# Weighing the sampled values: stationary pages or stationary probabilities

## The reference, cut to what matters

```
s = einsum('bqhd,bqkhd->bqhk', q, k_sel) * HEAD_DIM ** -0.5     # k_sel: chosen past tokens and the new one
p = softmax(where(valid, s, -inf))
o = einsum('bqhk,bqkhd->bqhd', p, v_sel)                        # per sample b and head h: 64 values
y = concatenate([o * silu(ga), ...])                            # then the output projection and the residual
```

## Time and profile before

| | us |
|---|---|
| median of 3 runs | 876.19 (873.66 to 878.19) |
| profiled execution | 876.71 |
| its span | 875.4 |
| TensorE matmul / weight load busy | 805.3 / 637.6 |
| VectorE / ScalarE / GpSimd busy | 609.3 / 328.0 / 333.1 |
| mean granted TensorE clock | 0.945 |

### The profile page before, as it was taken

How to read it: one execution, slowest core, us unless ns; L and a number is a source line. 1 busy time by engine, 2 the same in 40 slices (tenths; PEclk the granted TensorE clock), 3 DMA queues, 4 the chain that set the end, 5 groups by cost and what they waited for, 6 DMA issues and landing times. The chain is left out here.

```text
span 875.4 us, 13288 instructions
## 1 busy us (share of the span) xinstructions
PE 805.3 (92%) x4620; PEld 637.6 (73%) x4620; DVE 609.3 (70%) x1432; ACT 328.0 (37%) x830; POOL 333.1 (38%) x317
## 2 busy tenths in 40 slices
PE   5898989999889899999998899899998889999998
PEld 4894635568767777789998655455877777678998
DVE  3546997999998974433444879989999898531122
ACT  3735335336653331223132444343484524122102
POOL 0033886934744700110110568886274373000000
PEclk9999989999889998999999999999999899799999
DMA  4533040314143633012134304002414154400212
GB/s 166 154 99 100 16 121 13 84 42 124 49 113 94 203 124 123 1 44 81 61 101 113 100 4 121 24 21 83 144 52 106 53 163 143 144 1 23 71 54 98
DMA packets 57283, 75.09 MB, mean 86 GB/s; under 512 B 13233, under 2 KB 32889, under 8 KB 57185
## 3 DMA queue, kind: packets, MB, share of 16 engines
q1 hardware_dynamic: 57106, 74.17, 27.7%
q10 hardware_dynamic: 111, 0.08, 0.0%
HBM read 67.26 MB, written 7.61 MB: 86 GB/s over the span
## 5 line engine op out<-in xcount | busy, mean ns | idle before, releaser
L1164 PE MATMUL R<-x_hi,W_r 128*128 128x268 f32 x448 | 141.1, 315 | 27.2 <-DVE yT L1668 7.9
L1148 PE MATMUL R<-W_r,x_hi 128*128 128x512 f32 (+3 forms) x320 | 127.8, 399 | 12.2 <-DVE W_r L1474 12.2
L1177 PE MATMUL R<-yT,W 128*128 128x268 f32 (+2 forms) x768 | 135.0, 335 | 2.4 <-DVE yT L1474 2.4
L1166 PE MATMUL R<-x_hi,W_r 128*128 128x268 f32 x448 | 136.0, 304 | 0.0
L1165 PE MATMUL R<-x_lo,W_r 128*128 128x268 f32 x448 | 135.7, 303 | 0.0
L1177 PEld LDWEIGHTS R<-yT,W 128*128 128x128 f32 x768 | 114.8, 201 | 16.0 <-DVE yT L1474 2.6
L1149 PE MATMUL R<-W_r,x_hi 128*128 128x512 f32 (+3 forms) x320 | 120.7, 377 | 0.0
L1164 PEld LDWEIGHTS R<-x_hi,W_r 128*128 128x128 f32 x448 | 92.2, 206 | 38.9 <-DVE yT L1668 11.9
L1150 PE MATMUL R<-W_r,x_lo 128*128 128x512 f32 (+3 forms) x320 | 120.3, 376 | 0.0
L1474 DVE SCALAR_TENSOR_TENSOR cc<-uext,params,cc 128x528 f32<-128x528 f32 x120 | 110.4, 965 | 0.0
L764 POOL TENSOR_TENSOR W_r<-W,W_r 128x1024 fp32r<-128x1024 f32 x28 | 66.4, 2380 | 88.8 <-ACT W_r L882 88.6
(11 more groups left out here) (232 smaller groups left out, 1408.5 us busy)
## 6 DMA issues: line engine op xcount, KB each, us to landing
W<-in_w_in SPq DMA_DIRECT2D x52, 512.0 KB, 4.2
KV<-in_cache_k SPq DMA_DIRECT2D x32, 256.0 KB, 2.8
W<-in_w_out SPq DMA_DIRECT2D x8, 1024.0 KB, 7.4
KV<-in_cache_v SPq DMA_DIRECT2D x32, 256.0 KB, 2.8
ubx<-qkv_rows SPq DMA_DIRECT2D x16, 256.0 KB, 3.7
zi<-z_rows SPq DMA_DIRECT2D x16, 196.0 KB, 3.6
W<-in_w_in SPq DMA_DIRECT2D x8, 296.0 KB, 3.4
out_new_k_prompt<-kz SPq DMA_DIRECT2D x8, 256.0 KB, 2.0
```

The lines of the kernel that those rows point to most:

```text
L1148: pe.matmul(out, x_hi[:, kc, rows], hi, start=(kc == 0), stop=False)
L1164: pe.matmul(out, hi[:, cols], x_hi[:, kc, toks], start=(kc == 0), stop=False)
L1166: m = pe.matmul(out, lo[:, cols], x_hi[:, kc, toks], start=False, stop=(kc == KC - 1))
L1177: m = pe.matmul(R[:, k, 0:hi - lo], W[:, slot(x), kc % 4, 128 * (u[1] % 4):128 * (u[1] % 4) + 128], yT[:, kc, lo:hi], start=(kc == 0), sto ...
```

## The change

The roles of the operands are swapped. The probabilities of one page of one sample become the stationary operand, 32 columns wide (8 heads and 24 columns of zeros), and the whole page, 512 columns, is the moving one. The output, all 8 heads of probabilities against all 512 value columns, lies on 32 partitions; four samples go to four groups of 32 partitions of one bank. There are four such steps in a layer, at 37, 39, 41 and 43, ahead of the step's other units: samples 0 to 3 with their first page, with their second, then samples 4 to 7 in the same way, in `A[:, 0]` in place of `A[:, 3]` for the first four. After the second and the fourth step VectorE multiplies the bank with a mask (`K_OWN`), so that row h keeps only head h's own 64 columns, and writes `own` to SBUF (steps 40 and 43). At step 44 TensorE sums over each sample's rows with `own` as stationary and four columns of ones (`K_SUM`) as moving, which also turns the result, and adds the products with the new values, now 64 columns at a time. The result is 32 columns, and VectorE gates it in one instruction at step 44. `pts`, `pd` and `own` get buffers of their own, and GpSimd zeroes `pts` once, in layer 0. Pages are loaded in the new order, four at a time after each step.

```diff
@@ constants @@
+    for j in range(4):
+        for h in range(HEADS):
+            c[32 * j + h, K_OWN + h] = c[32 * j + h, K_SUM + j] = 1
@@ kv_load @@
-                    sp.wait_ge(*spv_s.at(n - 19))
-                src = a[name][l:l + 1, bass.ds(pages[n % 16], 1)].rearrange("a b p h d -> (a b p) (h d)")
+                    sp.wait_ge(*spv_s.at((n - 16) // 4))
+                page = n if n < 16 else 2 * (4 * ((n - 16) // 8) + n % 4) + (n - 16) // 4 % 2
+                src = a[name][l:l + 1, bass.ds(pages[page], 1)].rearrange("a b p h d -> (a b p) (h d)")
@@ pool_layer @@
+                pz_s.did(pool.memset(pts[:], 0.0))
@@ tensor_layer @@
+            def weigh_pages(t):
+                q, g = divmod(t, 2)
+                if t == 0:
+                    pe.wait_ge(*spk_s.at(2))
+                elif t == 2:
+                    pe.wait_ge(*PTk_s.at(len(ITEMS) - HEADS - 1))
+                for j in range(4):
+                    page, b = 16 + 4 * t + j, 4 * q + j
+                    pe.wait_ge(*kv_s[j].at(16 * (page // 4 + 1)))
+                    m = pe.matmul(A[32 * j:32 * j + 32, (3, 0)[q], :], pts[:, g, b, :], KV[:, j, :], start=(g == 0), stop=(g == 1))
+                spv_s.did(m)
+            def weigh_pages_sum():
+                pe.wait_ge(*pk_s.at(2))
+                pe.wait_ge(*rows_s.at(32))
+                for q in range(2):
+                    for c in range(4):
+                        pe.matmul(A[:, 3, 8 * c + 4 * q:8 * c + 4 * q + 4], own[:, q, 128 * c:128 * c + 128], cst[:, K_SUM:K_SUM + 4],
+                                  start=(q == 0 and c == 0), stop=False, skip_group_check=True)
+                for k in range(2):
+                    for c in range(4):
+                        new = pd[:, :].rearrange("p (b h) -> p b h", b=8)[:, :, 2 * c + k]
+                        m = pe.matmul(A[64 * k:64 * k + 64, 3, 8 * c:8 * c + 8],
+                                      rows8[:, 1024 + 128 * c + 64 * k:1024 + 128 * c + 64 * k + 64], new,
+                                      start=False, stop=(k == 1 and c == 3), skip_group_check=True)
+                px_s.did(m)
@@ tensor_layer, in the step @@
-                if SX["pv"] <= n < SX["pv"] + 8:
-                    acc = A[:, 3, 0:64]
-                    if n == SX["pv"]:
-                        for c in range(4):
-                            pe.matmul(acc[:, 16 * c:16 * c + 16], rows8[:, 1024 + 128 * c:1152 + 128 * c], new, ...)
-                    b = n - SX["pv"]
-                    for g in range(2):
-                        page = 16 + 2 * b + g
-                        pe.wait_ge(*kv_s[page % 4].at(16 * (page // 4 + 1)))
-                        for c in range(4):
-                            m = pe.matmul(acc[:, 16 * c + 2 * b:16 * c + 2 * b + 2], KV[:, page % 4, 128 * c:128 * c + 128],
-                                          pts[:, g, 8 * b + 2 * c:8 * b + 2 * c + 2], ...)
-                        spv_s.did(m)
+                if n in PV_STEPS:
+                    weigh_pages(PV_STEPS.index(n))
+                if n == PV_SUM:
+                    weigh_pages_sum()
@@ vector_layer @@
+                if n in PV_KEEP:
+                    q = PV_KEEP.index(n)
+                    dve.wait_ge(*spv_s.at(2 * q + 2))
+                    pk_s.did(dve.tensor_tensor(own[:, q, :]..., A[:, (3, 0)[q], :]..., cst[:, K_OWN:K_OWN + HEADS]..., ALU.mult))
                 if n == SX["gate"]:
-                    dve.wait_ge(*spv_s.at(16))
-                    for k in range(2):
-                        ys_s.did(stt(dst, src, 0.5, dst))
+                    dve.wait_ge(*px_s.at(1))
+                    ys_s.did(stt(dst, A[:, 3, 0:32].rearrange("p (c b) -> p c b", c=4), 0.5, dst))
```

More of the change, by code:

```diff
@@ L132 @@
 K_ID, K_ROT, K_CNT, K_WIN, K_E, K_ET, K_TRI = 0, 128, 128 + 48 * NT, 160 + 48 * NT, 162 + 48 * NT, 226 + 48 * NT, 234 + 48 * NT
-K_END = K_TRI + MAXR
+K_OWN, K_SUM = K_TRI + MAXR, K_TRI + MAXR + HEADS
+K_END = K_SUM + 4
 ACC_END = len(PIECES) + 4
@@ L151 @@
 SD = {"isc": 3, "logit_in": 29, "negmax": 31, "etp": 34}
+PV_STEPS, PV_KEEP, PV_SUM = (37, 39, 41, 43), (40, 43), 44
 SX = {"pool_diff": 9, "pool_diff2": 10, "ln_diag": 12, "ln_mul": 16, "ln_tanh": 17, "pages": 18, "swish": 20, "index": 26,
-      "index_turn": 27, "topk": 28, "logits": 32, "exp": 33, "norm": 34, "turn": 35, "keep": 36, "pv": 37, "ahead": 41, "gate": 45}
+      "index_turn": 27, "topk": 28, "logits": 32, "exp": 33, "norm": 34, "turn": 35, "keep": 36, "pv": 37, "ahead": 41, "gate": 44}
 def constants():
@@ L267, in program @@
         KV = sb("KV", 128, 4, 512)
+        pts = sb("pts", 128, 2, N_SAMPLE, 32)
+        pd = sb("pd", N_SAMPLE, 64)
+        own = sb("own", 128, 2, 512)
         rows8 = qkT[0:8, :, :].rearrange("p a b -> p (a b)")[:, 0:3 * 512]
@@ L286, in program @@
         wbc = smp[:, 256:320]
-        pts = smp[:, 320:448].rearrange("p (g x) -> p g x", g=2)
         sn = p64[:, 0:64]
-        pd = p64[:, 64:128]
         qb = ubx[:, :, :].rearrange("p a b -> p (a b)")[:, 0:1024].rearrange("p (a b) -> p a b", a=2)
@@ L512, in program @@
         MV_s = stage("meta_pv_done")
+        pz_s, pk_s, px_s = stage("s_probs_zeroed"), stage("s_pv_kept"), stage("s_pv_summed")
         store_s, row_q, row_k, row_v, row_z = queue("stored"), queue("q_row_kept"), queue("k_row_kept"), queue("v_row_kept"), queue("z_row_kept")
@@ L1079, in scalar_layer @@
                     act.wait_ge(*spt_s.at(1))
-                    spk_s.did(copy(pts[:, :, :], A[:, 3, 0:128].rearrange("p (g x) -> p g x", g=2)))
+                    if l == 0:
+                        act.wait_ge(*pz_s.at(1))
+                    spk_s.did(copy(pts[:, :, :, 0:HEADS], A[:, 3, 0:128].rearrange("p (g b h) -> p g b h", g=2, b=8)))
                     spk_s.did(copy(pd[:, :], A[0:8, 3, 128:192]))
@@ L1443, in tensor_layer @@
                         unit(u)
-                if SX["pv"] <= n < SX["pv"] + 8:
-                    acc = A[:, 3, 0:64]
-                    if n == SX["pv"]:
-                        pe.wait_ge(*spk_s.at(2))
-                        pe.wait_ge(*rows_s.at(32))
-                        for c in range(4):
-                            new = pd[:, :].rearrange("p (b h) -> p b h", b=8)[:, :, 2 * c:2 * c + 2]
-                            pe.matmul(acc[:, 16 * c:16 * c + 16], rows8[:, 1024 + 128 * c:1152 + 128 * c], new,
-                                      start=(c == 0), stop=False, skip_group_check=True)
-                    b = n - SX["pv"]
-                    for g in range(2):
-                        page = 16 + 2 * b + g
-                        pe.wait_ge(*kv_s[page % 4].at(16 * (page // 4 + 1)))
-                        for c in range(4):
-                            m = pe.matmul(acc[:, 16 * c + 2 * b:16 * c + 2 * b + 2], KV[:, page % 4, 128 * c:128 * c + 128],
-                                          pts[:, g, 8 * b + 2 * c:8 * b + 2 * c + 2], start=False,
-                                          stop=(page == 31 and c == 3), skip_group_check=True)
-                        spv_s.did(m)
             pe.wait_ge(*y_s.at(3))
-            pe.wait_ge(*ys_s.at(2))
+            pe.wait_ge(*ys_s.at(1))
             for m in range(KC):
@@ L1876, in vector_layer @@
                         split_rest(dve, l + 1, m, next_lo)
-                if n == SX["gate"]:
-                    dve.wait_ge(*spv_s.at(16))
-                    for k in range(2):
-                        rows = slice(64 * k, 64 * k + 64)
-                        dst = yT[rows, 0:4, NTOK:TOK]
-                        src = A[rows, 3, 0:64].rearrange("p (c b k) -> p c b k", c=4, b=8)[:, :, :, k]
-                        ys_s.did(stt(dst, src, 0.5, dst))
+                if n in PV_KEEP:
+                    q = PV_KEEP.index(n)
+                    dve.wait_ge(*spv_s.at(2 * q + 2))
+                    pk_s.did(dve.tensor_tensor(own[:, q, :].rearrange("p (h d) -> p h d", h=HEADS),
+                                               A[:, (3, 0)[q], :].rearrange("p (h d) -> p h d", h=HEADS),
+                                               cst[:, K_OWN:K_OWN + HEADS].unsqueeze(2).broadcast_to([128, HEADS, HD]), ALU.mult))
+                if n == SX["gate"]:
+                    dve.wait_ge(*px_s.at(1))
+                    dst = yT[:, 0:4, NTOK:TOK]
+                    ys_s.did(stt(dst, A[:, 3, 0:32].rearrange("p (c b) -> p c b", c=4), 0.5, dst))
                 if n < len(PLAN):
```

## The result

| | before | after |
|---|---|---|
| median of 4 runs each | 875.86 us | 849.67 us (848.39 to 854.95) |
| profiled execution | 876.71 | 854.95 |
| span of it | 875.4 | 853.6 |
| mean granted clock in it | 0.945 | 0.950 |

The ratio is 0.9707 with a 95% interval of 0.9657 to 0.9757; two later comparisons gave 0.9748 (0.9683 to 0.9813) and 0.9705 (0.9645 to 0.9766). Of the kernel before, 10 of the 45 later runs took more than 1.5% longer than the fastest beside them (up to 891 us), and these are left out of all ratios and means. The change makes the kernel 2.9% faster, about 26 us, where 1.6% was forecast, with the range ending at 857.

A forecast was written before the change was run, and what follows sets the result against it. TensorE's matmuls, busy 92% of the span, bound the kernel. A layer -15.0 + 5.2 + 3.5 = -6.3, two -12.6; gaps +0.4, layer 0's waits +0.8, clock -2.5: -13.9, from 876.7 to 863 us; 8 in 10 within 857 to 880.

The forecast's parts named there:

- What goes: Old page passes and new-value products on TensorE: 0.99 + 1.98 + about 12.0 = 15.0 us a layer removed.
- Four steps: New page products on TensorE: 1.3 us a step (bounds 1.0 and 3.7), 5.2 us a layer.
- the two bunches: Sign of being right: a step's eight page passes start in two bunches, next matmul 1.0 to 1.5 us after the first.
- The 0.3 us put down for starting eight loads and passes: Part of each page step's 1.3 us: up to 0.3 us for starting its eight loads and passes.
- The second and third rival: Page steps: second, passes start in program order, 871 us, chance 0.20; third, nothing runs side by side, 881 us, chance 0.20.
- the first: Rival on page loads: full concurrency but the four pages land late, +4.5 us, 867 us; chance 0.10.
- The sum: Sum over samples on TensorE: own 1.7, new values 1.6, shape changes 0.2, 3.5 us a layer; bounds 2.7 (halves side by side), 4.2.
- the 64-column row: Profile row pricing the sum's new-value products: two passes in 0.20 us, so 16 x 0.10 = 1.6 us.
- The 0.2 us for changes of shape: Allowance in the sum over samples: 0.2 us a layer for two changes of shape.
- Gaps and layer 0: TensorE's wait before the output projection's last third: 1.4 instead of 1.2 us, +0.2 a layer; layer 0's waits +0.8 us.
- The clock: Falls to 1.2 GHz behind the old sparse passes: 3.9 us may come back; 2.5 us gain taken, bounds -3 and +5.
- The fear that the new sum brings a fall of its own: Output units behind the sum's four- and eight-column passes: a clock fall there would cost up to 1.6 us each layer.

The follow-up runs named there:

- before_quarter: Kernel before with three quarters of the page products left out, 4 passes in each page group instead of 16: 847.4 us, ratio 0.9675.
- full_width: Changed kernel without column groups: stationary operand 128 columns wide, so every page pass takes the whole array (output not the samples'): 867.5 us, ratio 0.9919.
- the first look: A further trace of the unedited kernel before, taken to see where its clock falls: 875.3 us.
- before_wide: Kernel before with 128 moving columns in place of 2 in each page product (sample output not computed rightly): 864.5 us, ratio 0.9884.
- the two other traces: The changed kernel run twice more, unedited: medians 852.58 and 850.43 us.
- split_sum: Changed kernel with the sum cut in two: own products of samples 0 to 3 and new values at step 42, the rest at 44: 849.2 us, ratio 0.9669.

## Why the prediction was right and wrong

The direction and the mechanism were right; the size was not, and the time fell outside the range.

- What goes, 15.0 us a layer: nearly right. Leaving out three quarters of the passes in before_quarter shortened the stretch by 19.8 us, 20.9 by the same price. At 0.103 a pass a layer's 128 page passes and the 0.99 us of new values are 14.2 us.
- Four steps, 1.3 us each: the mechanism was right, the price was not. A step takes 0.99 to 1.00 us, my lower bound, and its passes start in the two bunches that I named as the sign. The 0.3 us put down for starting eight loads and passes isn't there: 4.0 instead of 5.2 us a layer. The choice of rows was sound: the transposes that overtook a score pass foretold that passes on free column groups don't wait for one whose group is busy, and full_width shows what it costs where nothing runs side by side. The second and third rival are refuted by the 1.0 us, and the first by the absence of any wait for a KV landing.
- By the Trainium skill ("TensorE: Matmul & The Clock Gate", Part 3, the mechanism), matmuls start in program order and a load overlaps a running matmul only where the row group differs. The trace disagrees with what would follow from both here: each sample's two passes stand next to each other in the program, and in-order starts would make at least 5 x 0.43 = 2.15 us a step, and the step takes 1.0 although all four groups share the rows; all eight loads start between 787.17 and 787.22 us, while the first passes run.
- The sum, 3.5 us a layer: measured 1.68 + 0.81 = 2.5, below my lower bound. The own products were right (1.7). The new-value products cost 0.05 us a pass, half of what the 64-column row gave. Most of that is not the side by side that I had held for possible (0.8) and not taken: within one half the passes start 0.06 us apart, 0.94 for sixteen, and the second half's begin when the first has three left, which saves the rest. The two passes of the row start 0.08 us apart; its 0.10 held the edge to the next matmul. The 0.2 us for changes of shape stands in no row, and none is seen.
- Gaps and layer 0: TensorE waits 1.48 and 1.41 instead of 1.22 us before the last third (+0.5 in both layers together) and 0.6 us for ScalarE's copy in layer 0. Both as forecast (+0.4, and 0.5 to 0.8).
- These terms together: with what was measured -28.4 + 8.0 + 5.0 + 0.5 + 0.6 = -14.3 us, and -14.6 by the stretch at the full clock; the forecast had -11.4.
- The clock, -2.5 us with +5 as the end: this step failed. In the stretch the falls cost 9.4 us before, in the mean of two traces, and 2.3 after: 7.1 us came back. I priced two falls, behind the first page group of each layer, at 3.9 us. The same profile has a third in the stretch, which the sum leaves out (windows of the kernel before; the granted clock is the seventh figure):

```profile
384.00:388.00 4.00, 4.00 (x12) 3.02 (x12) 0.28 (x2) 0.00 (x0) 0.00 (x0) 0.59 0.10 39
394.00:398.00 4.00, 4.00 (x24) 4.00 (x23) 1.12 (x4) 0.90 (x3) 0.00 (x0) 0.57 0.05 19
```

  With it the falls were 6.8 us in that profile, not 3.9, and the first look has 11.9. The sparse stretches of two-column passes in all eight steps could each bring the clock down, and in other executions did; before_wide shows it with the same number of passes. The fear that the new sum brings a fall of its own was right: the profile has it in both layers, the two other traces in layer 0.

Of the 13.3 us beyond the forecast in the medians, 3.2 are thus passes and waits (steps and sum, less what the old passes were overpriced) and 4.6 the clock in the stretch. The other 5.5 are not located; falls elsewhere in the program and the scatter of the runs can hold them. The measured 14.6 and the clock's bound of +5 give 857 us, the end of the range; what puts the time below it is the 2.1 us by which the clock in the stretch passed that bound, and those 5.5. The profiled execution of the kernel after (854.95) was itself the longest of its four.

## What to carry to other kernels

Where few columns of moving data meet wide stationary blocks, swap the operands and put independent products on separate column groups: four cost what one does, also where each product is two passes next to each other. Passes with a handful of moving columns cost more than their own time, as the units behind them may run at half the clock; price them over several traces or by a variant that only widens them, since one trace can show the mildest case. To split a gain between work and clock, measure the changed stretch in the trace and its time at 1.2 GHz; the time of the whole times its mean clock blames the clock for too much. Where rows put a bound on a term from below, don't add an allowance that no row shows.

## What the runs showed of the hardware that was not expected

- Sixteen passes of two columns and sixteen of 128 take nearly the same time in the old kernel (1.83 and 1.93 us from the first start to the next matmul's in layer 0's second group), but the granted clock of the steps around them was 0.93, 0.88 and 0.80 in three traces with the first and 1.00 in three with the second, 11.5 us of the whole by the means.
- Eight fp32 passes of 512 columns on four column groups take 1.0 us; on the whole array 3.5.
- Sixteen passes with 64 stationary columns and 8 moving ones, in two halves of the array, take 0.81 us together, 0.05 each; within one half they start 0.06 apart, where passes with 128 stationary columns and 4 moving ones start 0.11 apart.
- 1.66 us of such passes at step 42 were followed by a fall of the granted clock in both layers (split_sum), with TensorE busy without a gap.
- Where in an execution the clock falls changes from run to run of the same kernel: the traces of the kernel before have 89 to 137 us at 1.2 GHz. Its runs differ by 2.6% (868 to 891 us), and one us more at 1.2 GHz goes with 0.35 us more of time.
